# One level of Strassen's scheme in the feed-forward in-products of a two-layer decoder step (Trainium2, one core)

## What is computed

```python
def swiglu(x, w_in, w_out):
    gate, up = jnp.split(x @ w_in, 2, axis=-1)
    return (jax.nn.silu(gate) * up) @ w_out
...
        h = h + 0.5 * swiglu(rms_norm(h, g[0]), P['ffn_w_in'][l, 0], P['ffn_w_out'][l, 0])
        xn = rms_norm(h, g[1])
...
        h = h + 0.5 * swiglu(rms_norm(h, g[2]), P['ffn_w_in'][l, 1], P['ffn_w_out'][l, 1])
```

## Time and profile before

| | |
|---|---|
| three runs | 2958.31, 2972.89, 2978.73 us |
| the profiled execution, its own time | 2960.64 us |
| its span, first to last instruction | 2959.0 us |
| PE busy | 2794.9 us, 94% of the span |
| DVE busy | 1185.8 us, 40% |
| ACT busy | 806.5 us, 27% |
| POOL busy | 282.6 us, 10% |
| granted clock of PE, mean over the span | 0.942 of full speed |

### The profile page before, as it was taken

The page is one execution under the profiler, slowest core; times in us unless marked ns, Lnnn a source line. Parts: engine busy times, 40 slices in busy tenths (PEclk is TensorE's granted clock), DMA queues, the critical chain, the costliest instruction groups (busy, mean ns, idle before and its releaser), DMA issues. The chain is left out here.

```text
span 2959.0 us, 56832 instructions
## 1 busy us (share of the span) xinstructions
PE 2794.9 (94%) x25177; PEld 2551.7 (86%) x25177; DVE 1185.8 (40%) x1738; ACT 806.5 (27%) x1261; POOL 282.6 (10%) x288
## 2 busy tenths in 40 slices
PE   7999969998999899999998989999998889999997
PEld 7999966776899746999997879999995568999997
DVE  4333355176333251433334123333444443433335
ACT  4212212132222100222221053212226762322221
POOL 1000000001111110000001200000007860000000
PEclk9999989999998557999998999999998997999998
DMA  6222210210000000322224622222222010222222
GB/s 233 82 89 86 77 64 15 71 58 30 4 3 4 33 29 26 131 82 80 95 69 120 162 100 85 85 100 85 71 74 65 23 44 29 88 90 79 99 69 75
DMA packets 36806, 214.84 MB, mean 73 GB/s; under 512 B 5232, under 2 KB 5360, under 8 KB 20880
## 3 DMA queue, kind: packets, MB, share of 16 engines
q1 hardware_dynamic: 27936, 174.34, 17.1%
q0 software_dynamic: 8720, 38.28, 4.4%
...
## 5 line engine op out<-in xcount | busy, mean ns | idle before, releaser
L518 PE MATMUL banks<-xh,wh 128*128 128x272 f32 x3072 | 638.7, 289 | 30.3 <-DVE wl L1484 18.0
L518 PE MATMUL banks<-xh,wl 128*128 128x272 f32 x3072 | 637.5, 289 | 0.0
L518 PE MATMUL banks<-xl,wh 128*128 128x272 f32 x3072 | 635.0, 288 | 0.0
L518 PEld LDWEIGHTS banks<-xh,wh 128*128 128x128 f32 x3072 | 485.5, 189 | 31.1 <-DVE wl L1484 23.4
L518 PEld LDWEIGHTS banks<-xl,wh 128*128 128x128 f32 x3072 | 484.7, 189 | 0.0
L518 PEld LDWEIGHTS banks<-xh,wl 128*128 128x128 f32 x3072 | 481.2, 189 | 0.0
L1484 DVE TENSOR_TENSOR wl<-raw,wh 128x2048 fp32r<-128x2048 f32 (+2 forms) x160 | 323.9, 2024 | 109.8 <-ACT wh L1133 109.7
L1133 ACT ACTIVATE wh<-raw 128x2048 fp32r<-128x2048 f32 (+2 forms) x160 | 270.7, 1692 | 260.5 <-PE banks L518 243.9
L518 PE MATMUL banks<-hh,wl 128*128 128x272 f32 x1408 | 291.4, 288 | 0.0
L518 PE MATMUL banks<-hh,wh 128*128 128x272 f32 x1408 | 291.0, 288 | 0.0
L518 PE MATMUL banks<-hl,wh 128*128 128x272 f32 x1408 | 290.2, 288 | 0.0
...
## 6 DMA issues: line engine op xcount, KB each, us to landing
...
```

Source lines behind the costliest of these rows:

```text
L518: ins = mm(pst[:, bank + half, 0:HALF], wt[:, s, w], a[:, half * HALF:(half + 1) * HALF], start=first, stop=last)
```

## The change

The in-product of a hidden tile is a matrix of 256 outputs (gate and up) by 1024 inputs, times 1024 by 544. The change cuts both into quarters, the weights as (gate, up) by (even, odd input tiles), the activations as (even, odd tiles) by (first, second half of the tokens), and makes the four quarters of the result from seven products of quarters in place of eight (the form of the scheme with 15 sums). Each of the seven is 4 tiles x 3 passes = 12 matmuls of 272 columns (`eighth`), so a slot is 84 matmuls. For that:

- POOL makes four sums of weight quarters for each slot (`weight_sums`, four subtractions or additions of 128x512, from `raw` and `sums_w`), and, once for each FFN, four sums of activation quarters for each of four pairs of tiles (`operand_sums`, 128x272 each).
- ACT and DVE split seven quarters of weights for a slot (3584 columns, in two steps, `weights_a` for three quarters that are weights themselves and `weights_s` for the sums) where they split four before (2048 columns); and seven quarters of activations for four. The split weights have one buffer now, `ring_h` and `ring_l`, whose parts are written again as soon as PE has used them.
- The products land in four banks x, y, w, z of a set. Some are taken out in the middle of a slot: ACT copies x to SBUF three times and z once (`snap`), and DVE makes the sums of products with six instructions of 272 columns.
- DVE waits for the gate's sum, scales it by `rr`, multiplies by up in two halves, and splits as before; the high and low copy of the hidden tile t are made after the first product of slot t+1 (`tail`).
- Since the operands' seven quarters take more room, a hidden buffer holds 6 tiles: an FFN has four in- and four out-stages, with 6, 6, 6 and 4 hidden tiles. The first two slots of an out-stage are interleaved on PE, and both end with their last tile's matmuls.
- DMAs that POOL issued early in an FFN stand behind its sums now.

PE and SyncE:

```diff
-FTA = 12
-FTB = FT - FTA
+FT_IN = (6, 6, 6, 4)
...
-            def out_stage(name, tiles, hidden):
+            def eighth(bank, quarter, f, b, js, start, stop):
+
+                for j in js:
+                    w = slice((4 * quarter + j) * P, (4 * quarter + j + 1) * P)
+                    xh_j, xl_j = xop_h[f][j][:, b, :], xop_l[f][j][:, b, :]
+                    for wt, x, first, last in ((ring_h, xh_j, start and j == 0, False), (ring_h, xl_j, False, False),
...
+                f = int(name[-1])
+                k0, _, ks = STAGES[name]
+                slot = IN_SLOTS[name] + s
+                x_bank, y_bank, w_bank, z_bank = range(4 * s, 4 * s + 4)
+                take_split(s, i + k0, i + ks)
...
+                else:
+                    eighth(y_bank, 1, f, 1, range(4), True, True)
+                    eighth(x_bank, 0, f, 0, range(4), True, True).then_inc(eighth_done, 1)
+                    eighth(w_bank, 2, f, 6, range(4), True, True).then_inc(eighth_done, 1)
+                pe.wait_ge(sums_split, i * 4 + (2 * slot + 1))
+                pe.wait_ge(snap, i * 8 + (4 * slot + 1))
+                eighth(x_bank, 3, f, 4, range(4), False, True).then_inc(eighth_done, 1)
+                if s == 0 and n is not None:
+                    norm(n, 4)
+                eighth(z_bank, 4, f, 3, range(4), True, True).then_inc(eighth_done, 1)
+                pe.wait_ge(snap, i * 8 + (4 * slot + 2))
+                eighth(x_bank, 5, f, 5, range(4), False, True).then_inc(eighth_done, 1)
+                pe.wait_ge(sums_split, i * 4 + (2 * slot + 2))
+                pe.wait_ge(snap, i * 8 + (4 * slot + 3))
+                eighth(z_bank, 6, f, 2, range(4), False, True).then_inc(multiplied[s], 1)
...
+            def out_stage(name):
 
                 k0, pairs, ks = STAGES[name]
-                with pe.Fori(0, pairs) as i:
+                f, tiles, hidden = int(name[-1]), FT_IN["ABCD".index(name[3])], hidden_before(name)
+
+                def tile(s, ft):
+                    return times(4 * s, s, ft, hh[f][:, ft, :], hl[f][:, ft, :], ft == 0, ft == tiles - 1)
+
+                for x in range(2):
+                    pe.wait_ge(hid_done[x], hidden + tiles // 2 - 1)
+                for s in range(2):
+                    take_split(s, k0, ks)
+                    for ft in range(tiles - 2):
+                        tile(s, ft)
+                pe.wait_ge(hid_done[0], hidden + tiles // 2)
+                for s in range(2):
+                    tile(s, tiles - 2)
+                pe.wait_ge(hid_done[1], hidden + tiles // 2)
+                for s in range(2):
+                    tile(s, tiles - 1).then_inc(multiplied[s], 1)
+                with pe.Fori(1, pairs) as i:
                     for s in range(2):
...
                         last.then_inc(multiplied[s], 1)
```

ACT and DVE in an in-stage:

```diff
+            def weights_s(name, t, used=lambda g: None):
+
+                n = IN_SLOTS[name] + t
+                act.wait_ge(sums, 2 * n + 1)
+                used(1)
+                act.activation(ring_h[:, 3 * QTR:6 * QTR], sums_w[:, 0:3 * QTR], ACT.Copy).then_inc(sums_hi, 1)
+                act.wait_ge(sums, 2 * n + 2)
+                used(2)
+                act.activation(ring_h[:, 6 * QTR:7 * QTR], sums_w[:, 3 * QTR:4 * QTR], ACT.Copy).then_inc(sums_hi, 1)
...
+            def operands(f, q, j):
+
+                stage_waits(act, f, j)
+                x = staged(f, j)
+                for t, out in ((2 * j, x[:, 0:8:7, :]), (2 * j + 1, x[:, 1:3, :])):
+                    act.activation(out, halves(hT[:, t, :]), ACT.Copy, scale=par(q, t)).then_inc(xg_done, 1)
+                act.wait_ge(xg_done, 8 * f + 2 * j + 2)
+                act.activation(xop_h[f][j][:, 0:3, :], x[:, 0:3, :], ACT.Copy).then_inc(xop_hi, 1)
+
+            def operand_sums(f, j):
+
+                act.wait_ge(xt_done, 4 * f + j + 1)
+                act.activation(xop_h[f][j][:, 3:7, :], staged(f, j)[:, 3:7, :], ACT.Copy).then_inc(xop_hi, 1)
...
+                for t in range(slots):
+                    s, k = t % 2, IN_SLOTS[name] + t
+                    x, z = pst[:, 4 * s, 0:HALF], pst[:, 4 * s + 3, 0:HALF]
+                    if hidden + t // 2:
+                        act.wait_ge(hid_done[s], hidden + t // 2)
+                    if t == 0 and n is not None:
+                        act.wait_ge(acc_step, EV * (n + 1))
+                    act.wait_ge(eighth_done, 5 * k + 1)
+                    act.activation(sg[:, s, 0:HALF], x, ACT.Copy).then_inc(snap, 1)
+                    if t:
+                        tail(t - 1)
+                    act.wait_ge(eighth_done, 5 * k + 2)
+                    if t + 1 < slots:
+                        weights_a(name, t + 1)
+                    else:
+                        out_weights(out, 0)
+                    act.wait_ge(eighth_done, 5 * k + 3)
+                    act.activation(sg[:, s, HALF:TOK], x, ACT.Copy).then_inc(snap, 1)
+                    if t == 0 and n is not None:
+                        norm(n, 4)
+                    act.wait_ge(eighth_done, 5 * k + 4)
+                    act.activation(up[1], z, ACT.Copy).then_inc(snap, 1)
+                    act.wait_ge(eighth_done, 5 * k + 5)
+                    act.activation(up[0], x, ACT.Copy).then_inc(snap, 1)
+                    if t + 1 < slots:
+                        weights_s(name, t + 1, lambda g, k=k, s=s, m=k0 + t // 2 + 1:
+                                  act.wait_ge(eighth_done, 5 * k + 5) if g == 1 else act.wait_ge(multiplied[s], m))
+                    else:
+                        out_weights(out, 1)
+                    act.wait_ge(gate_scaled[s], hidden + t // 2 + 1)
+                    act.activation(sg[:, s, :], sg[:, s, :], ACT.Silu).then_inc(gate_done[s], 1)
+                tail(slots - 1)
...
+            def weights_s(name, t, part):
+
+                n, c = IN_SLOTS[name] + t, (slice(3 * QTR, 6 * QTR), slice(6 * QTR, 7 * QTR))[part]
+                dve.wait_ge(sums_hi, 2 * n + part + 1)
+                dve.tensor_tensor(ring_l[:, c], sums_w[:, c.start - 3 * QTR:c.stop - 3 * QTR],
+                                  ring_h[:, c].bitcast(F32), ALU.subtract).then_inc(sums_split, 1)
+
+            def low_operands(f, j, part):
+
+                c = (slice(0, 3), slice(3, 7))[part]
+                dve.wait_ge(xop_hi, 8 * f + order_of(f, j, part) + 1)
+                dve.tensor_tensor(xop_l[f][j][:, c, :], staged(f, j)[:, c, :],
+                                  xop_h[f][j][:, c, :].bitcast(F32), ALU.subtract).then_inc(xop_split, 1)
...
+                for t in range(slots):
+                    s, k, h = t % 2, IN_SLOTS[name] + t, hidden + t // 2 + 1
+                    x, y, w, z = (pst[:, 4 * s + n, 0:HALF] for n in range(4))
+                    g0, g1 = sg[:, s, 0:HALF], sg[:, s, HALF:TOK]
+                    dve.wait_ge(snap, 4 * k + 1)
+                    do(dve.tensor_tensor(g0, y, g0, ALU.add))
+                    if t:
+                        tail(t - 1)
+                    if t + 1 < slots:
+                        weights_a(name, t + 1)
+                    else:
+                        split(out, 0, 0)
+                    if t == 0 and before:
+                        before()
+                    dve.wait_ge(snap, 4 * k + 4)
+                    dve.tensor_tensor(up[1], x, up[1], ALU.add).then_inc(up_done, 1)
+                    dve.tensor_tensor(up[0], w, up[0], ALU.add).then_inc(up_done, 1)
+                    dve.wait_ge(multiplied[s], k0 + t // 2 + 1)
+                    dve.tensor_tensor(g1, z, g1, ALU.add).then_inc(taken[s], 1)
+                    own.wait()
+                    dve.wait_ge(taken[s], k0 + t // 2 + 1)
+                    dve.tensor_tensor(sg[:, s, :], sg[:, s, :], rr[:], ALU.mult).then_inc(gate_scaled[s], 1)
+                    if t + 1 < slots:
+                        weights_s(name, t + 1, 0)
+                    else:
+                        split(out, 0, 1)
+                    dve.wait_ge(gate_done[s], h)
+                    dve.wait_ge(up_done, 2 * k + 2)
+                    dve.tensor_tensor(sg[:, s, 0:HALF], sg[:, s, 0:HALF], up[0], ALU.mult)
+                    dve.tensor_tensor(sg[:, s, HALF:TOK], sg[:, s, HALF:TOK], up[1], ALU.mult)\
+                       .then_inc(hid_ready[s], 1)
+                    if t + 1 < slots:
+                        weights_s(name, t + 1, 1)
+                tail(slots - 1)
```

POOL:

```diff
+            def operand_sums(f, j):
+
+                x = staged(f, j)
+                b11, b21, b22, t1, t2, t3, t4, b12 = (x[:, n, :] for n in range(8))
+                pool.wait_ge(xg_done, 8 * f + 2 * j + 1)
+                pool.tensor_tensor(t1, b12, b11, ALU.subtract).then_inc(t_step, 1)
+                pool.wait_ge(xg_done, 8 * f + 2 * j + 2)
+                pool.wait_ge(t_step, 8 * f + 2 * j + 1)
+                pool.tensor_tensor(t2, b22, t1, ALU.subtract).then_inc(t_step, 1)
```

(22 more changed lines are left out.)

422 lines of the change are left out of this document (283 added, 139 removed).

## The result

| | before | after |
|---|---|---|
| median of the runs beside each other | 2975.81 us (2958.31 to 2988.57, 4 runs) | 3077.08 us (3049.16 to 3079.88, 4 runs) |
| span of the profiled execution | 2959.0 us | 3074.0 us |
| PE busy | 94% | 89% |

The change makes the kernel slower: the ratio is 1.0323, with a 95% interval from 1.0243 to 1.0404. I had forecast 2998 us and a range from 2920 to 3050, so the sign that I called likelier was right and the size was a quarter of the real one.

A forecast was written before the change was run, and what follows sets the result against it. PE's matmuls were taken to bound the kernel; -126.3 + 43 (port) + 47 (out-stages) + 2 (`q`'s operands) + 53 (starts) + 6 (clock) gave +25 us, a median of 2998 us, range 2920 to 3050.

The forecast's parts named there:

- the sign that I called likelier: Whole execution: slower by over 1%, chance 0.45, against 0.19 for faster by over 1%.
- What bounds the kernel, and what is removed: PE bounds the kernel at 125.3 ns a matmul; 12 of 96 matmuls go in each of 88 slots.
- the term of -126 us: In-stage slots behind each FFN's first: 12 matmuls fewer in 84 slots, -126.3 us.
- Rival C: In-stage slots: seven products cost more than their count, 5 ns a matmul, +37 us on the sum; chance 0.05.
- DVE in a slot, POOL and the port: Steady in-stage slot: DVE's 7.8 us plus 3.3 us held up by POOL's sums, 11.1 us; +43 us for four FFNs.
- rival B: In-stage slots: POOL and DVE take more, 1.35 us a sum, 11.7 us a slot, +71 us, median 3044; chance 0.22.
- Out-stages: Out-stages of four FFNs: PE waits for weight splits, the last hidden tile and `outD`'s slots, +47 us.
- The wait ahead of the third slot: Out-stages: PE waits 1.9 us for the third slot's split, in three stages an FFN.
- the 3.1 and the 0.6: Last out-stage, `outD`: 3.1 us of wait for the split behind a square, 0.6 us for the last hidden tile.
- the five waits of 0.5: `outD`: PE's slot is 3.0 us; scale, add, square and split take about 3.5, so five waits of 0.5 us.
- the clock: Starts of the four FFNs: new pauses of 4 to 17 us each cost half of a half-clock stretch, +6 us.
- Starts: First slots of FFNs 0 to 3 end later by 17.5, 8.2, 19.4 and 8.2 us, +53 us together.

The follow-up runs named there:

- experiment 6: The kernel before with two input tiles of the up part left out, 84 matmuls a slot for 96: 2828.7 us beside a median of 2968.0.
- (1): The changed kernel with POOL making only 16 of 512 columns of each weight sum from each FFN's second slot on: 2990.3 us beside 2951.5 before.
- experiment 3: The changed kernel with the four weight sums of a slot made by DVE and not POOL: ratio 1.0104 to the kernel before.
- (4): The kernel with the weight sums on DVE, with the operands' sums moved from POOL to DVE too: ratio 1.0105 to the kernel before.
- experiment 10: All sums on DVE, skewed out-stage order, stages of 4, 6, 6, 6 tiles, plus four of FFN 0's squares moved earlier: ratio 0.988 to the kernel before.

## Why the prediction was wrong

**What bounds the kernel, and what is removed.** Right. PE's pace is the same (12 matmuls in 1.50 us), and experiment 6 gives the term of -126 us as computed. Rival C, a price for the seven products themselves, is out: at 10.50 us a slot costs its 84 matmuls and nothing more.

**DVE in a slot, POOL and the port.** The mechanism was right, and it decides: with POOL's time taken away (1) or its work on DVE (3) the slot is PE's 10.5 us again. The size was wrong by half a microsecond a slot. I wrote "3.3 us, and 7.8 + 3.3 = 11.1 us for a steady slot"; it is 4.0 + 7.6 = 11.6. DVE's own work is 0.2 less than I took. The waits are 0.7 more, since I let each sum overlap the start of DVE's instruction or one with an input in PSUM (0.9, 0.9, 0.55 and 0.9 us of each 1.2), while in the trace POOL's next sum stands ready when DVE's instruction ends and takes the port, so that DVE's next is held for 1.09 of POOL's 1.27. That is rival B's slot of 11.7 us, for which I had given 0.22, by its cause (DVE is never idle, so all counts) and nearly by its price for a sum (1.35 us; the median of line 2355 is 1.36). The term is 59.4 us for 43.

**A term that was not in the sum.** I costed the port only inside in-stages. At the end of an out-stage, POOL's sums of the next in-stage's first slot meet DVE's line 1878 and the split of line 1753 that PE is about to need: 1.2 to 1.5 us, twelve times, 16.1 us. Experiments 1 and 3 take it to nothing.

**Out-stages.** The wait ahead of the third slot was costed at 1.9 us and is 1.93. In the last stage the 3.1 and the 0.6 are met too (3.12 and 0.61; 3.99 in FFN 2), and the five waits of 0.5 are larger: 3.3 us together, in FFN 2 5.3, since a slot of 24 matmuls comes every 3.75 to 4.7 us. That DVE and ACT need that long for scale, add, square and split is my reading. Pauses are 56.5 us for 47, of which 1.9 are the wait for weights in FFN 0. What failed most is the clock: I charged it once at each start and never behind a pause in an out-stage, and 19.8 us are that, half of them behind pauses of 1.9 us and half behind those of 3.1 and 4.0.

**Starts.** They were to grow by 17.5, 8.2, 19.4 and 8.2 us with 6 for the clock, and grew by 23.2, 11.1, 24.0 and 11.3. The places were right: FFN 2's first slot falls from 37.7 us to 28.6 when the weight sums leave POOL (experiment 3) and to 23.4 when the operand sums do (4), and experiment 10 shows ACT's squares ahead of product four. FFN 2's sum also ends with 6.3 us for the 48 matmuls and the small product, for which the others have 7.1. The time of one sum of 272 columns, 0.76 for the 0.7 I took, is 1 us of it at FFN 2; where DVE interferes it is up to 1.83, and I had charged 0.4 for each.

**The rest.** 12 us of the profiled execution, and an unknown part of the 101 us between the medians, lie in the recurrence, and its time varies by 22 us among profiles of kernels with the same code there. I can't say that the change causes any of it. Experiments 3 and 4 have the same remainder: their FFNs take 1595 and 1584 us, no more than the 1595.5 before, and still they are 1.0% slower than before, with 809 and 799 us for the recurrence in their profiles. So what they lose stands outside the FFNs, as far as one profile of each can tell, and why is open.

In short, six terms erred to the same side, none by more than 20 us. Most of it hangs on two sources: an exclusive port in front of an engine that never rests, and a clock that falls behind short pauses. The range left no room for that, because I took the ends of POOL's duration as the only unknown, and each term's waits as independent of the others.
